# A two-block transformer kernel in three-product fp16: norm sums by token, one joint norm, pooling from the widest window down, and half of the gates' low part on ScalarE

## Chip, cores, metric

One core of one Trainium2 chip. The metric is device time in microseconds of one execution. The kernel is written at the level of engines: TensorE (PE), VectorE (DVE), ScalarE (ACT), GpSimd (POOL) and SyncE (SP), which starts most transfers. Each has its own program, and semaphores order them.

## What is computed

512 tokens of width 1024 go through two blocks, in fp32. Cut to what matters:

```python
# first block
h = concat(meta, x)                        # 16 + 512 tokens
proj = rmsnorm(h, ln1_w) @ w_in            # attention, gated linear attention
h = h + concat(attention, gla) @ w_out     # then the 512 tokens alone
hn = rmsnorm(h, ln2_w)
h = h + peer_ffn(hn)                       # top 16 of 128*128 experts, 8 heads, by token
x = rmsnorm(h, final_norm_w)               # "final1"
# second block
h = rmsnorm_2(x, mix_norm)                 # "mixn"
z = h @ w_in_2                             # pool, u, v and two gates, 1024 columns each
y_a = pool_mixer(z_pool) @ w_branch_a      # mean over the last 2, 4, 8, 16 tokens by channel group
y_b = (gelu(u) * (ws @ rmsnorm_2(gelu(v)) + b)) @ w_branch_b
x = x + (g_a * y_a + g_b * y_b) @ w_out
x = x + conv_ffn(rmsnorm_2(x, ffn_norm))   # "ffnn"
x = x + sigmoid(rmsnorm_2(x, ple_norm) @ w_gate) * (p @ w_ple)   # "plen"
return rmsnorm_2(x, final_norm)            # "final2"

rmsnorm(x, w) = x * rsqrt(mean(x*x, axis=-1) + 1e-6) * w
pool_mixer:  group g of 256 channels, w = (2, 4, 8, 16)[g]:
             (sum of the last w tokens) / min(t+1, w) - z, then @ w_pool[g], * pool_scale
```

## The kernel before

**Layout.** X holds the residual stream with channels on the 128 partitions: 8 chunks (c) of 128 channels, tokens along the free side (512, or 528 with the meta tokens). Weights come in slabs of 128x1024 fp32 through a ring of four (`wraw`): ScalarE cuts each to its fp16 high part (`cut_high`, L498), VectorE to the low part (`cut_low`, L511); in the expert part GpSimd takes the low cut for a while. Both ask for slab n+3 before they handle what slab n gave. A product of fp32 quality is three fp16 products, high by high, high by low, low by high (`parts`, L537 to L539). A chunk of a projection is 24 of them, 512 columns wide.

**Norms** (`class Norm`). ScalarE squares the chunks (L393) and loads the root's table ahead of the last one. TensorE sums over channels: with `ones` as weights and the squares moving (ln1, L421, L422), or for the others with `strip` as weights, which puts the sums of token tile t on rows 32t to 32t+31 (L426), four products of 128 columns a chunk. ScalarE takes the root (L400), on 128x128 or, for ln1, 128x528. VectorE takes the reciprocal (L452, L455), TensorE spreads it over all partitions (L445; not for ln1), and VectorE scales X (L461), from which ScalarE copies the high part (L406) and VectorE takes the low (L467). For ln2, ffnn and final2 GpSimd adds the squares of the first six chunks beforehand (L438). The final norm of block one writes X itself, and the first norm of block two starts from its squares.

**Experts.** All 128x128 experts are computed densely for 384 tokens, in 128 slabs; 128 tokens' picks are gathered instead. The matrix of gates is built in 48 octets of tokens, in six tile turns of eight octets and five slabs each: VectorE writes one-hot codes of column and row (`hot_slab`, `hot_row`, L2061, L2062) and the first times the gate's high and low half (L2064, L2065), in two buffers used in turn; TensorE multiplies them (`gate_octet`, L1119, L1120), ScalarE copies the result out (L1603), and at the end of a turn starts the store of 4096 KB to `gate_matrix`. Between octets TensorE takes half slabs (`spilled`), whose Gelu ScalarE writes (L1561). Then groups of four value slabs are accumulated in all eight banks of PSUM (`expert_output`); the last slab's products of chunk c are followed by a transpose of the gathered tokens' sum (L1148), and VectorE adds bank c to X (L2159).

**After it.** Norms final1 and mixn, then eight pool projections (`N_POOL`), four slabs of pool weights (`N_WP`), eight of gating values v in two halves (`N_SV`), eight of u (`N_SU`). A pool chunk c is evicted by ScalarE (L1672) into one of two buffers, GpSimd adds c//2+1 shifted copies (L2373), VectorE divides, subtracts and cuts (L2180 to L2184, L2170, L2171); ScalarE's next eviction but one waits for that. The pooled products' outputs are evicted and cut in the same way (L1679, L1682, L2191). SP's queue starts all slab transfers in order, with two small weights behind the end of final1.

What sets the order is the text of the five programs alone; nothing reorders them.

Of the kernel before, what the change touches and what calls it, by code (L numbers as in the profile page):

```python
# [49 lines left out]
N_WP = N_POOL + 8  # L50
N_SV = N_WP + 4
N_SU = N_SV + 8
# [69 lines left out]
def build(nc, io, out):  # L122
# [3 lines left out]
    with ctx:  # L126
# [32 lines left out]
        strip = base.take(P + 96)  # L159
# [164 lines left out]
        consts_in, vecs_in, ones_in, meta_in = sem("consts_in"), sem("vecs_in"), sem("ones_in"), sem("meta_in")  # L324
# [42 lines left out]
        POOLED, FIRST = ("ln2", "ffnn", "final2"), 6  # L367
        squares_added = sem("squares_added")
        NORMS = ("ln1", "ln2", "final1", "mixn", "ffnn", "plen", "final2")
# [5 lines left out]
        class Norm:  # L375


            def __init__(self, name, b):
                self.i = NORMS.index(name)
                self.b = b  # L380
                self.w, self.meta = VEC[name], name == "ln1"
                self.cut = name not in ("final1", "final2")
                self.nth = sum(n not in ("final1", "final2") for n in NORMS[:self.i])
                self.cols = TM if self.meta else T

                self.pooled = POOLED.index(name) if name in POOLED else None
                self.sq = nsq1 if self.meta else xsq if name == "final1" else nsq
                self.std = nstd1 if self.meta else nstd
                self.inv = ninv1 if self.meta else ninv

            def square(self, c):

                nc.scalar.activation(self.sq[:, c, 0:self.cols], X[:, c, 0:self.cols],  # L393
# [4 lines left out]
            def act(self, act, meanwhile=lambda: None):  # L398
                act.wait_ge(ss_done, self.i + 1)
                nc.scalar.activation(self.std, bank(self.b, TM if self.meta else P), ACT.Sqrt, bias=EPSC,  # L400
                                     scale=1.0 / D).then_inc(std_done, 1)
                meanwhile()
                if self.cut:
                    for c in range(KC):
                        act.wait_ge(xn_done, self.nth * KC + c + 1)
# [3 lines left out]
            def sum(self, pe, c):  # L409
# [3 lines left out]
                if self.pooled is not None and c < FIRST:  # L413
                    if c < FIRST - 1:
                        return
                    pe.wait_ge(squares_added, (self.pooled + 1) * (FIRST - 1))
                    c, first = 0, True
                else:
                    pe.wait_ge(sq_act, self.i * KC + c + 1)
                if self.meta:  # L420
                    nc.tensor.matmul(bank(self.b), ones, self.sq[:, c, 0:T], start=c == 0, stop=c == KC - 1)  # L421
# [347 lines left out]
        def _(pe):  # L769
# [394 lines left out]
            for c in range(KC):  # L1164
                n3.sum(pe, c)
# [1330 lines left out]
```

## Time and profile before

| | |
|---|---|
| median of 3 runs | 2467.96 us (2465.28 to 2469.02) |
| the profiled execution | 2466.73 us |
| its span | 2465.0 us |
| busy: PE, DVE, ACT, POOL | 95%, 69%, 43%, 25% of the span |
| HBM traffic | 190 GB/s over the span |

How to read the rows further down. In a timeline a row is: start and length in us, engine (PE is a product, SPq and ACTq a transfer's issue), line, operation, output<-input, shapes, xN for N in a row; in brackets the idle time before and who ended it. A list by line ends in the count, then busy us, mean ns | idle before, releaser. A row of one line's instructions gives ns min/median/max, then first and last start. A row of windows is the stretch, its length, then busy us (count) of PE, PE's weight loads, DVE, ACT, POOL, then the mean granted clock of TensorE (1.00 is 2.4 GHz), the DMA engines' share and GB/s. An fp32 product appears as two PE instructions.

### The profile page before, as it was taken

To read this page: it belongs to the slowest core of one execution; us is meant where nothing else is said; L and a number is where in the kernel's file an instruction comes from. 1 tells how busy PE (TensorE), PEld (TensorE's weight loads), DVE (VectorE), ACT (ScalarE), POOL (GpSimd) and SP (SyncE) were. 2 spreads that over 40 slices of the span, in tenths; PEclk is the share of its full clock that TensorE was granted. 3 is DMA by queue.
4 is the path that set the end of the run, shared out by engine and by line. 5 is a ranking of instruction groups with operands and counts; after the bars stand their busy time and mean duration, and the time that the engine had idled before them with its cause. 6 is when DMAs were issued, how large, how long until landed. Compare 5 with 4: busy or idle time off the path is not lost.

```text
span 2465.0 us, 38176 instructions
## 1 busy us (share of the span) xinstructions
PE 2336.5 (95%) x13568; PEld 1302.4 (53%) x13568; DVE 1707.9 (69%) x2979; ACT 1050.0 (43%) x1496; POOL 612.7 (25%) x494
## 2 busy tenths in 40 slices
PE   7998788999999998989999999988999999999998
PEld 3446664555555566655555555563454444443453
DVE  5326674568899989987888888878353438777235
ACT  4255333565666664543333333344422224333234
POOL 0003361277677651123322222204000010000001
PEclk9998999999999999999999999999999999999999
DMA  5200003378788778889999999923233323332321
GB/s 177 77 26 1 1 1 102 124 263 302 279 302 319 253 226 320 331 305 362 389 361 362 359 362 362 363 95 94 86 112 103 101 77 105 102 102 94 103 85 52
DMA packets 164871, 470.79 MB, mean 191 GB/s; under 512 B 17616, under 2 KB 70736, under 8 KB 163984
## 3 DMA queue, kind: packets, MB, share of 16 engines
q1 hardware_dynamic: 109312, 289.59, 34.3%
q0 software_dynamic: 36864, 134.23, 14.8%
q10 hardware_dynamic: 18576, 45.36, 4.9%
q8 instruction: 77, 1.26, 0.2%
q14 instruction: 42, 0.34, 0.0%
HBM read 421.67 MB, written 47.45 MB: 190 GB/s over the span
## 4 chain that ended last, share of the span: by engine, by line
PE 74%; DVE 14%; issue 4%; POOL 3%; ACT 2%; DMA 2%; DVEq 1%; SPq 0%; POOLq 0%; ACTq 0%
PE psum L537 23%; PE psum L538 23%; PE psum L539 23%; DVE arena L2026 3%; POOL arena L682 2%; PE psum L426 1%; DMA arena<-in_urows,arena 1%; DVE arena L2064 1%; DVE arena L511 1%; DVE arena L2061 1%; DVE arena L2065 1%; POOL arena L517 1%; DVEq L1951 1%; DVE arena L1868 0%; POOL arena L2335 0%
## 5 line engine op out<-in xcount | busy, mean ns | idle before, releaser
L537 PE MATMUL psum<-arena 128*128 128x384 f16 (+3 forms) x3648 | 1261.5, 347 | 34.2 <-DVE arena L467 13.2
L538 PE MATMUL psum<-arena 128*128 128x384 f16 (+3 forms) x3648 | 1264.6, 347 | 0.0
L539 PE MATMUL psum<-arena 128*128 128x384 f16 (+3 forms) x3648 | 1258.0, 346 | 0.0
L537 PEld LDWEIGHTS psum<-arena 128*128 128x128 f16 (+1 forms) x3648 | 354.1, 97 | 366.0 <-issue 50.5
L539 PEld LDWEIGHTS psum<-arena 128*128 128x128 f16 (+1 forms) x3648 | 353.9, 97 | 324.0 <-issue 8.1
L538 PEld LDWEIGHTS psum<-arena 128*128 128x128 f16 (+1 forms) x3648 | 353.6, 97 | 312.0 <-issue 8.4
L511 DVE SCALAR_TENSOR_TENSOR arena<-arena 128x1024 f16<-128x1024 f32 x216 | 267.4, 1240 | 307.9 <-ACT arena L498 307.4
L498 ACT ACTIVATE arena<-arena 128x1024 f16<-128x1024 f32 x216 | 226.4, 1050 | 259.5 <-PE psum L539 243.0
L1619 ACT ACTIVATE arena<-arena 128x1024 f16<-128x1024 f32 x128 | 135.3, 1057 | 298.9 <-PE psum L539 282.8
L517 POOL TENSOR_TENSOR arena<-arena 128x1024 f16<-128x1024 f32 x104 | 214.7, 2064 | 108.3 <-ACT arena L506 106.6
L2335 POOL DMA_INDIRECT arena<-in_v,arena x128 | 133.0, 1039 | 355.4 <-DVE arena L2037 323.6
L438 POOL TENSOR_TENSOR arena<-arena 128x512 f32<-128x512 f32 x15 | 19.8, 1320 | 760.3 <-ACT arena L393 760.3
L2335 POOL DMA_INDIRECT arena<-in_urows,arena x128 | 133.8, 1046 | 213.2 <-DVE arena L2026 156.3
L2026 DVE CUSTOM_DVE_ANT_0 arena<-arena,psum 128x1024 f32<-128x1024 f32 x128 | 151.3, 1216 | 26.4 <-DMA arena<-in_urows,arena 25.0
L2037 DVE SCALAR_TENSOR_TENSOR arena<-arena 128x1024 f32<-128x1024 f32 x126 | 161.0, 1280 | 0.0
L2111 DVE SCALAR_TENSOR_TENSOR arena<-arena 128x1024 f16<-128x1024 f32 x128 | 156.1, 1220 | 0.0
L1561 ACT ACTIVATE arena<-psum 128x384 f32<-128x384 f32 x128 | 62.8, 491 | 168.1 <-PE psum L539 160.4
L2105 DVE TENSOR_TENSOR arena<-arena 128x384 f16<-128x384 f32 x128 | 71.4, 558 | 63.0 <-ACT arena L1624 60.4
L504 ACT ACTIVATE arena<-arena 128x1024 f16<-128x1024 f32 x104 | 109.0, 1048 | 10.5 <-DMA arena<-in_w 9.9
L506 ACT ACTIVATE arena<-arena 128x1024 f32<-128x1024 f32 x104 | 110.0, 1058 | 3.3
L682 POOL TENSOR_TENSOR arena<-arena 64x256 f32<-64x256 f32 x72 | 63.3, 879 | 95.6 <-ACT arena L1456 92.2
L1727 ACT ACTIVATE arena<-psum 128x512 f32<-128x512 f32 x44 | 26.3, 598 | 142.5 <-PE psum L539 142.5
(254 smaller groups left out, 2236.9 us busy)
## 6 DMA issues: line engine op xcount, KB each, us to landing
arena<-in_w SPq DMA_DIRECT2D x320, 512.0 KB
arena<-in_v SPq DMA_DIRECT2D x128, 512.0 KB
early_activations<-arena ACTq DMA_DIRECT2D x124, 192.0 KB
arena<-early_activations SPq DMA_DIRECT2D x124, 192.0 KB
gate_matrix<-arena ACTq DMA_DIRECT2D x5, 4096.0 KB, 16.0
arena<-gate_matrix SPq DMA_DIRECT2D x32, 640.0 KB
arena<-in_xT SPq DMA_DIRECT2D x4, 512.0 KB, 5.5
arena<-in_urows,arena POOLq DMA_INDIRECT x128
```

The costliest lines, as they stand in the source:

```text
L498: nc.scalar.activation(wh[:, s, :], wraw[:, s, :], ACT.Copy, scale=WS).then_inc(high_cut, 1)
L511: nc.vector.scalar_tensor_tensor(out=wl[:, s, :], in0=wraw[:, s, :], scalar=WS, in1=wh[:, s, :], op0=ALU.mult, op1=ALU.subtract).then_inc( ...
L517: nc.gpsimd.tensor_tensor(wl[:, s, :], wraw[:, s, :], wh[:, s, :], ALU.subtract).then_inc(low_cut, 1)
L537: nc.tensor.matmul(ps, a_h, b_h, start=first, stop=False)
L538: nc.tensor.matmul(ps, a_h, b_l, start=False, stop=False)
L539: return nc.tensor.matmul(ps, a_l, b_h, start=False, stop=last)
L682: do.tensor_tensor(blocks(dst[li][rows, :], s, sd), blocks(src[rows, h, 0:T], s, sd), blocks(e[rows, :], s, sd), ALU.mult).then_inc(done, 1)
L1619: nc.scalar.activation(vh[:, s, :], vraw[:, s, :], ACT.Copy, scale=WS).then_inc(vhigh_cut, 1)
L2026: nc.vector.tensor_tensor_reduce(out=x, in0=x, in1=own_tok, scale=1.0, scalar=0.0, op0=ALU.mult, op1=ALU.add, accum_out=own_dot[:, k:k + 1 ...
L2037: ins = nc.vector.scalar_tensor_tensor(out=to, in0=x, scalar=by, in1=to, op0=ALU.mult, op1=ALU.add)
L2111: nc.vector.scalar_tensor_tensor(out=vl[:, s, :], in0=vraw[:, s, :], scalar=WS, in1=vh[:, s, :], op0=ALU.mult, op1=ALU.subtract).then_inc( ...
L2335: nc.gpsimd.indirect_dma_start(own_row(b, k >= PICKS), None, table, bass.IndirectOffsetOnAxis(own_at[:, k % PICKS:k % PICKS + 1], 0)).then ...
```

## The change

- **Sums by token.** The squares are now the weights and a table of a few columns (`pick`) moves: the sums of token tile t land with tokens on the partitions in column t. Roots and reciprocals are of 128x4 (128x5 for ln1, 128x8 joint), and the spread uses the reciprocal's column as broadcast weights with the identity moving. ln1, which had no spread, gets one; VectorE adds its squares 3 to 7. `pick` and the identity are loaded ahead of the other x, `ones` behind.
- **A joint norm.** From x = h*r1*w1 the second norm's moment is r1^2 * mean(h^2 w1^2): both means come from one pass over the squares of h, with two columns a tile (`wpick`). VectorE forms s1+eps and eps*(s1+eps)+s2 and their reciprocals, ScalarE one root of the eight. X is scaled with both at once for mixn; the scaling for the residual follows later, in the first step of the pooling loop.
- **Dealt sums.** The sums of chunk c-2 follow chunk c's products of the last value slab.
- **Pooling descending**: channel group 3 (window 16, four shifted sums) first; the first half of the gating values is placed between the pool projections and the pooled products, and the pooled products' outputs use another buffer (U2).
- **The gates' low part.** VectorE writes the first four tokens of an octet, ScalarE the other four with one scaled copy each (`low_half`), one octet ahead; TensorE waits for both.

```diff
@@ Norm @@
+        ADDED = {"ln1": (3, 7), "ln2": (0, 5), "ffnn": (0, 5), "final2": (0, 5)}
...
             def act(self, act, meanwhile=lambda: None):
-                act.wait_ge(ss_done, self.i + 1)
-                nc.scalar.activation(self.std, bank(self.b, TM if self.meta else P), ACT.Sqrt, bias=EPSC,
-                                     scale=1.0 / D).then_inc(std_done, 1)
+                if self.double:
+                    act.wait_ge(std_done, self.i + 1)
+                    nc.scalar.activation(self.inv, self.std, ACT.Sqrt).then_inc(inv_done, 1)
+                else:
+                    act.wait_ge(ss_done, self.i + 1)
+                    nc.scalar.activation(self.std, bank(self.sums, self.n), ACT.Sqrt, bias=EPSC,
+                                         scale=1.0 / D).then_inc(std_done, 1)
...
-                    for t in range(TT):
-                        last = nc.tensor.matmul(bank(self.b, P), strip[:, 96 - 32 * t:96 - 32 * t + P],
-                                                self.sq[:, c, t * P:(t + 1) * P], start=first and t == 0,
-                                                stop=c == KC - 1 and t == TT - 1)
...
+                for t in (0, *range(TT, self.tiles), *range(1, TT)):
+                    rows = P if t < TT else M
+                    w = wpick[:, c, 6 - 2 * t:14 - 2 * t] if self.double else pick[:, TT - t:TT - t + self.n]
+                    last = nc.tensor.matmul(bank(self.sums, self.n)[0:rows], self.squares[:, c, t * P:t * P + rows], w,
+                                            start=first and t == 0, stop=end and t == TT - 1)
...
+            def spread(self, pe):
+
+                pe.wait_ge(inv_done, self.i + 1)
+                for at, b in ((TT, self.b), (0, self.b - 1)) if self.double else ((0, self.b),):
+                    for t in range(self.tiles):
+                        rows = P if t < TT else M
+                        last = nc.tensor.matmul(psum[:, b * 512 + t * P:b * 512 + t * P + rows],
+                                                self.inv[0:rows, at + t:at + t + 1].to_broadcast([rows, P]),
+                                                ident[0:rows, 0:rows], start=True, stop=True)
+                    last.then_inc(spread_done, 1)
...
+                if self.double:
+                    dve.wait_ge(ss_done, self.i + 1)
+                    s1, s2 = (bank(self.sums, self.n)[:, j:self.n:2] for j in range(2))
+                    dchain.link(nc.vector.tensor_scalar(moments[:, 0:TT], s1, EPS, None, ALU.add))
+                    dchain.link(nc.vector.scalar_tensor_tensor(out=moments[:, TT:2 * TT], in0=moments[:, 0:TT], scalar=EPS,
+                                                               in1=s2, op0=ALU.mult, op1=ALU.add))
+                    nc.vector.reciprocal(self.std, moments).then_inc(std_done, 1)
@@ TensorE @@
...
                 pe.wait_ge(hot_out, e + 1)
+                pe.wait_ge(low_out, e + 1)
...
                         nc.tensor.transpose(bank(c, P, ND), own_sum[0][:, cols], ident).then_inc(own_turned, 1)
+                        if c >= 2:
+                            n4.sum(pe, c - 2)
...
-            n3 = Norm("final1", 0)
-            for c in range(KC):
-                n3.sum(pe, c)
-            n3.spread(pe)
-
-            n4 = Norm("mixn", 7)
-            for c in range(KC):
+            for c in (KC - 2, KC - 1):
                 n4.sum(pe, c)
             n4.spread(pe)
...
+            pe.wait_ge(final1_out, KC)
+            gating_values(N_SV)
+            pe.wait_ge(zpool_out, KC)
+            for n in range(N_WP, N_SV2):
...
+            pe.wait_ge(v_out, TT)
+            gating_values(N_SV2)
@@ ScalarE @@
+            def low_half(e):
+
+                b = e % 2
+                act.wait_ge(hot_slab_out, e + 1)
+                wait(act, g_done, e * 2 - 2)
+                for j in range(OCT // 2, OCT):
+                    tok = e * OCT + j
+                    last = nc.scalar.activation(hot_low[b][:, j // QUAD, :, j % QUAD],
+                                                hot_slab[b][:, j // QUAD, :, j % QUAD], ACT.Copy,
+                                                scale=idxT[:, 2, tok:tok + 1])
+                last.then_inc(low_out, 1)
+
+            low_half(0)
...
                     cuts.upto(N_U + e + (i + i // 4 + (i % 4 == 3)) // 2 + 3)
+                    if t * OCT + i + 1 < GT * OCT:
+                        low_half(t * OCT + i + 1)
@@ VectorE @@
+            n1.add_squares(dve, nc.vector)
...
-            cuts.upto(2)
-            n1 = Norm("ln1", 0)
-            n1.dve(dve)
+            cuts.upto(1)
+            n1.dve(dve, meanwhile=lambda: cuts.upto(2))
...
-                nc.vector.tensor_tensor(hot_low[b], hot_slab[b], col(gatel), ALU.mult).then_inc(hot_out, 1)
+                half = OCT // QUAD // 2
+                nc.vector.tensor_tensor(hot_low[b][:, 0:half], hot_slab[b][:, 0:half], col(gatel)[:, 0:half],
+                                        ALU.mult).then_inc(hot_out, 1)
...
+            for n in range(N_POOL, N_SV):
+                p, c = n - N_POOL, N_SV - 1 - n
                 cuts.upto(n + 3)
...
+                if n == N_POOL:
+                    dve.wait_ge(spread_done, n4.i + 2)
+                    for cc in range(KC):
+                        nc.vector.scalar_tensor_tensor(out=X[:, cc, 0:T], in0=X[:, cc, 0:T], scalar=f1[:, cc:cc + 1],
+                                                       in1=bank(n4.b - 1), op0=ALU.mult,
+                                                       op1=ALU.mult).then_inc(final1_out, 1)
```

The order of the instructions at two places, L numbers being those of each version's own lines. First TensorE at the end of the last value slab, before the change; L537 to L539 are products, L1148 the transpose, L426 sums, L445 spreads:

```order
L537 MATMUL psum<-arena 128x384
L538 MATMUL psum<-arena 128x384
L539 MATMUL psum<-arena 128x384
L1148 MATMUL psum<-arena 128x128
L426 MATMUL psum<-arena 128x128 x32
L445 MATMUL psum<-arena 128x128 x4
L426 MATMUL psum<-arena 128x128 x32
L445 MATMUL psum<-arena 128x128 x4
L537 MATMUL psum<-arena 128x512
```

And with the change, where L553 to L555 are the products, L1170 the transpose, L434 sums and L454 spreads:

```order
L434 MATMUL psum<-arena 128x8 x4
L553 MATMUL psum<-arena 128x384
L554 MATMUL psum<-arena 128x384
L555 MATMUL psum<-arena 128x384
L1170 MATMUL psum<-arena 128x128
L434 MATMUL psum<-arena 128x8 x12
L454 MATMUL psum<-arena 128x128 x8
L553 MATMUL psum<-arena 128x512
```

Four sums of each earlier chunk now stand before the next chunk's products, twelve behind the last transpose, and the second pass of 32 is gone.

Second ScalarE in the first tile turn, before: L1603 copies gates out, L1550 stores an activation, L1561 is the Gelu, L498 the high cut:

```order
L1603 ACTIVATE arena<-psum 128x128x4 x4
L1550 DMA early_activations<-arena 128x384
L1561 ACTIVATE arena<-psum 128x384
L498 ACTIVATE arena<-arena 128x1024
L1603 ACTIVATE arena<-psum 128x128x4 x2
```

And with the change, L1621 being the scaled copies, L1639 the gates out, L514 the cut:

```order
L1621 ACTIVATE arena<-arena 128x128 x4
L514 ACTIVATE arena<-arena 128x1024
L1621 ACTIVATE arena<-arena 128x128 x4
L1639 ACTIVATE arena<-psum 128x128x4 x2
L1621 ACTIVATE arena<-arena 128x128 x4
L1639 ACTIVATE arena<-psum 128x128x4 x2
```

Each octet's gates are copied out behind the scaled copies for the octet after it.

## Rows read from the trace of the kernel before

**Rows 1.** The page, part 4: the chain that ended last, its share by engine.

```profile
PE 74%; DVE 14%; issue 4%; POOL 3%; ACT 2%; DMA 2%; DVEq 1%; SPq 0%; POOLq 0%; ACTq 0%
```

**Rows 2.** TensorE's waits: who was waited for, us in total, times, longest.

```profile
PE psum L1119 <- DVE arena L2065: 19.9, 23, 1.6
PE psum L537 <- DVE arena L2191: 5.1, 1, 5.1
```

**Rows 3.** The timeline of the start: start us, length us, instruction, [idle before <-releaser].

```profile
10.83 0.15 DVE L1787 TENSOR_TENSOR arena<-arena 64x2 f32<-64x2 f32 x1 [10.83 <-DMA arena<-in_vec]
12.57 0.63 ACT L393 ACTIVATE arena<-arena 128x528 f32<-128x528 f32 x1
16.22 0.29 PE L422 MATMUL psum<-arena 128*128 128x16 f32 x2
17.30 0.29 PE L422 MATMUL psum<-arena 128*128 128x16 f32 x2
18.71 0.70 ACT L400 ACTIVATE arena<-psum,arena 128x528 f32<-128x528 f32 x1 [2.68 <-PE psum L422]
19.45 3.45 DVE L452 RECIPROCAL arena<-arena 128x528 f32<-128x528 f32 x1 [1.67 <-ACT arena L400]
22.94 1.45 DVE L461 SCALAR_TENSOR_TENSOR arena<-arena 128x528 f32<-128x528 f32 x2
25.27 0.58 PE L537 MATMUL psum<-arena 128*128 128x512 f16 x1 [6.29 <-DVE arena L467]
```

**Rows 4.** The tile stage: one turn's busy times, VectorE's L2065, ScalarE's copies by shape.

```profile
955.40:987.00 31.60, 28.25 (x252) 19.34 (x250) 30.77 (x48) 15.89 (x26) 5.72 (x5) 1.00 0.89 330
...
L2065 DVE TENSOR_TENSOR arena<-arena x48: 678/685/2481, 896.2 to 1088.7; 128x1024 f16<-128x1024 f16 x48
...
L1603 ACT ACTIVATE arena<-psum 128x512 f32<-128x512 f32 x80 | 44.8, 617 | 22.4 <-PE psum L1120 22.4
L1561 ACT ACTIVATE arena<-psum 128x384 f32<-128x384 f32 x25 | 12.3, 491 | 36.2 <-PE psum L539 34.9 <-issue 1.3
```

**Rows 5.** The lines L400, L455, L2194: duration ns min/median/max.

```profile
L400 ACT ACTIVATE arena<-psum,arena x7: 367/368/702, 18.7 to 2453.9; 128x128 f32<-128x128 f32 x6, 128x528 f32<-128x528 f32 x1
...
L455 DVE RECIPROCAL arena<-arena x6: 952/953/954, 446.1 to 2454.3; 128x128 f32<-128x128 f32 x6
...
L2194 DVE RECIPROCAL arena<-arena x1: 180/180/180, 1775.5 to 1775.5; 128x4 f32<-128x4 f32 x1
```

**Rows 6.** The timeline between the last expert slab and the pool projections.

```profile
1634.44 7.31 PE L426 MATMUL psum<-arena 128*128 128x128 f32 x64
1635.42 1.28 ACT L373 ACT_TABLE_LOAD   x1
1643.19 1.16 PE L445 MATMUL psum<-arena 128*128 128x128 f32 x8 [1.45 <-DVE arena L455]
1644.39 5.36 DVE L461 SCALAR_TENSOR_TENSOR arena<-arena,psum 128x512 f32<-128x512 f32 x8 [1.25 <-PE psum L445]
1655.91 1.41 DVE L461 SCALAR_TENSOR_TENSOR arena<-arena,psum 128x512 f32<-128x512 f32 x2 [1.25 <-PE psum L445]
```

**Rows 7.** The pooling part: windows, lines L2171 and L2373, and the timeline.

```profile
1670.90:1767.20 96.30, 89.24 (x393) 38.82 (x392) 59.62 (x67) 37.77 (x50) 26.59 (x21) 0.95 0.34 108
1716.70:1729.00 12.30, 12.30 (x46) 5.05 (x47) 7.93 (x10) 6.10 (x10) 0.00 (x0) 0.79 0.46 144
...
L2171 DVE TENSOR_TENSOR arena<-arena x46: 691/693/1644, 1675.0 to 2270.8; 128x512 f16<-128x512 f32 x26, 128x512 f32 x20
...
L2373 POOL TENSOR_TENSOR arena<-arena x20: 1062/1270/1916, 1671.6 to 1708.7; 128x527 f32<-128x527 f32 x8, 128x525 f32<-128x525 f32 x6, 128x521 f32<-128x521 f32 x4, 128x513 f32<-128x513 f32 x2
...
1697.13 1.23 DVE L511 SCALAR_TENSOR_TENSOR arena<-arena 128x1024 f16<-128x1024 f32 x1
1703.87 1.23 DVE L511 SCALAR_TENSOR_TENSOR arena<-arena 128x1024 f16<-128x1024 f32 x1
...
1704.59 0.39 PE L537 MATMUL psum<-arena 128*128 128x512 f16 x1 [2.00 <-ACT arena L1672]
```

More of the change, by code:

```diff
@@ L366, in build @@
         xn_done, xh_done, xl_done = sem("xn_done"), sem("xh_done"), sem("xl_done")
-        POOLED, FIRST = ("ln2", "ffnn", "final2"), 6
         squares_added = sem("squares_added")
-        NORMS = ("ln1", "ln2", "final1", "mixn", "ffnn", "plen", "final2")
+        NORMS = ("ln1", "ln2", "mixn", "ffnn", "plen", "final2")
+        ADDED = {"ln1": (3, 7), "ln2": (0, 5), "ffnn": (0, 5), "final2": (0, 5)}
         def roots_table(i):
@@ L441, in spread @@
-            def spread(self, pe):
-                pe.wait_ge(inv_done, self.i)
-                for t in range(TT):
-                    last = nc.tensor.matmul(bank(self.b, P, t * P), ident[:, 32 * t:32 * t + 1].to_broadcast([P, P]),
-                                            self.inv, start=True, stop=True)
-                last.then_inc(spread_done, 1)
-            def dve(self, dve, dst=None, done=None):
-                dve.wait_ge(std_done, self.i + 1)
-                if self.meta:
-                    dchain.link(nc.vector.reciprocal(self.inv, self.std))
-                    inv = self.inv
-                else:
+                end = c == KC - 1 or c == self.lo and self.hi == KC - 1
@@ L1136, in _ @@
                 spilled(e)
+            n4 = Norm("mixn", 7, sums=0)
             def expert_output(n, s, first=False, last=False):
@@ L1654, in _ @@
             cuts.upto(N_POOL + 2)
-            n3, n4 = Norm("final1", 0), Norm("mixn", 7)
+            n4 = Norm("mixn", 7, sums=0)
             for c in range(KC):
                 act.wait_ge(acc_out, c + 1)
-                n3.square(c)
-            n3.act(act)
-            for c in range(KC):
-                act.wait_ge(final1_out, c + 1)
                 n4.square(c)
@@ L1673, in _, with gating_values_out @@
                                      scale=ISW).then_inc(zpool_out, 1)
-            for n in range(N_WP, N_SV):
+            def gating_values_out(lo, half):
+                cuts.upto(lo + 7)
+                act.wait_ge(slab_done, lo + 4)
+                for t in range(TT):
+                    nc.scalar.activation(V2[:, 2 * t + half, :], bank(4 + t), ACT.Gelu,
+                                         scale=ISW).then_inc(v_out, 1)
+            gating_values_out(N_SV, 0)
+            for n in range(N_WP, N_SV2):
@@ L2160, in _ @@
                                                op0=ALU.mult, op1=ALU.add).then_inc(acc_out, 1)
-            Norm("final1", 0).dve(dve, dst=X, done=final1_out)
-            Norm("mixn", 7).dve(dve)
+            n4 = Norm("mixn", 7, sums=0)
+            n4.dve(dve)
             nc.vector.tensor_scalar(PSC, vec[:, VEC["pscale"]:VEC["pscale"] + KC], ISW, None,
```

250 lines of the change are left out of this document (129 added, 121 removed).

## The prediction

> **What bounds the kernel now.** I read the page first, then TensorE's waits, then the timeline of the four places that the change touches. The chain that ended last is 74% TensorE [rows 1], so a microsecond is worth something only where TensorE stands still, runs at half clock, or works for nothing. Its list of waits [rows 2] names two such places: 19.9 us in 23 waits before the gates' products (L1119, VectorE late), and one wait of 5.1 us in the pooling part. The other idle time is in the norms: at the start TensorE waits 6.29 us for the first operand [rows 3], and between the last expert slab and the pool projections the two norms take from 1634.44 until the second scaling starts at 1655.91 [rows 6], 21.5 us with no large product. In the tile stage [rows 4] VectorE is busy 30.77 of 31.6 us, ScalarE 15.89: VectorE sets that pace, ScalarE has half its time free.
>
> The sum is made against the profiled execution, 2466.73 us (span 2465.0 and 1.7 around it). The median of the runs, 2467.96, lies 1.2 higher; I add that at the end.
>
> **Part 1, the start: 4.2 us gained.** Before: last square done at 13.2, sums until 18.7, a square root over 528 columns (0.70), a reciprocal of 3.45 us, first scaling at 22.94 [rows 3]. A cycle there, 17.30-16.22 = 1.08 us, holds an fp32 product of 512 columns and one of 16, two instructions each. Of it 0.85 us is the 512 columns (2 instructions of 2 x 512 columns at 2.4 GHz); 0.23 is left for the two narrow ones, 0.117 each. I take 0.117 for every narrow fp32 instruction with new weights. After: VectorE gets its vectors at 10.8, does five tiny ones (0.8 us) and adds four squares (0.7 each), the last after the square at 13.2: 14.6. The sum product of 5 tiles is 10 instructions, 1.2 us: 15.8. Meanwhile VectorE does two slab cuts (2.3 us) until 17.0 and only then the reciprocal, 0.18 like the small one in [rows 5]. The spread is a step that was not there: 10 instructions of 1.16/8 = 0.145 [rows 6] and a start, 1.6 us, 18.7; the third cut (1.2 us) lies beside it. First scaling 18.75 instead of 22.94. The identity matrix is now asked for ahead of the remaining x (64 KB more in that queue, 0.2 us); the constants land long before the rotation that needs them. Bounds: 2.5 (cuts and adds late) and 6 (less half clock in the first products).
>
> **Part 2, the smaller norm operands: 3.6 us.** For ln2, ffnn, plen and final2 the reciprocal falls from 0.95 to 0.18 us on 128x4, the root from 0.37 to about 0.3 [rows 5]; 0.85-0.9 us each, times 4, all of it between the sums and the spread where TensorE stands. The sums themselves stay: 8 narrow instructions of 0.117 are 0.94 us, and 64 instructions took 7.31 us before, 0.914 per chunk [rows 6]. Bounds 2.5 and 4.5.
>
> The first rows show that what limits the new sums is the weight load, since the columns are gone. The Trainium skill, "TensorE: Matmul & The Clock Gate", section "Weight-path perf modes", says that fast weight load does not apply to fp32, and the section on LDWEIGHTS gives P/1.2 ns, 107 ns for 128 columns. By that rule a chunk's sums cost 0.86 us instead of 0.94, and turning the squares into weights buys nothing on TensorE.
>
> **Part 3, the joint norm: 11.1 us.** Now the eight chunks' sums start at 1634.44 and end at 1641.75, TensorE-bound; with them between the products the same work is there. Each chunk of the last slab takes 0.60 us (three products of 384 columns at 2.4 GHz, 0.48, and a transpose, 0.12) plus 0.94 of sums from the third on. Sum 0 waits for its square (0.4 us). Chunk 7's transpose then ends near 1639.5, sum 5 at 1640.5, accumulation and square of chunk 7 come behind the table load of 1.28 us [rows 6] at 1641.5, and the last sum ends at 1642.5. **Dealing the sums loses 0.8 us.** Three small VectorE operations (0.55), the root (0.3) and the first spread (1.2) follow: the scaling for mixn starts at 1644.8, where the one for final1 started at 1644.39. The second scaling started at 1655.91: 11.1 us less. What vanishes there is 5.36 us of scaling X, the second squares, 7.4 us of sums, root, reciprocal. The second spread (1.2 us) ends before the first low part of X is cut, and X's scaling (5.4 us) moves behind the cuts, into the time before the first window sum is out. Bounds 9.5 and 12.5.
>
> **Part 4, the gates' low part: 9.5 us.** VectorE's fourth operation takes 0.685 us for 1024 columns [rows 4]; less the overlap of neighbours (eight scalings of 0.74 in 5.36 us [rows 6], so 0.08) its pitch is 0.60, and 0.33 for 512, so 0.27 times 48 octets = 13 us less on VectorE. ScalarE gets four of 128 columns. Its price: 0.617 us for 512 and 0.491 for 384 columns [rows 4] give 0.24 for 128; the root with a pointer operand on 128x128 takes 0.37 [rows 5]; neighbours overlap by about 0.08 again. I take 0.30, 1.2 us a group, 9.6 a tile turn: 25.5 of about 29.8 us. At the first octet ScalarE reaches its group only after the preceding slab's Gelu: 1.2-1.9 us lost once. TensorE's own work bounds a turn: 31.6 less 19.9/6 = 3.3 of waits [rows 2, 4] is 28.3; VectorE's 30.77 less 2.16 is 28.6. With both that close they will wait for each other in turn, as VectorE's 0.83 us of idle time shows already, so I take 29.8 a turn; 1.8 times 6, less 1.3. Bounds 0 and 12. Two more things queue: behind ScalarE's new wait for the slab one-hots stand its gate copies and the Gelu, which have two octets of slack in banks; DMA at a share of 0.89 [rows 4] would be 0.95.
>
> By the Trainium skill, "ScalarE: Activation LUTs", section "Rules for kernel authors", multiplication belongs on VectorE. The rows bear it out, 1.2 us for what costs 0.27, and applied to a path through ScalarE it would cost 0.93 times 48 = 45 us. The trace's idle half of ScalarE is why I don't follow it.
>
> **Part 5, pooling in descending order: 4.2 us.** Before, TensorE lost 2.00 us [rows 7] and 5.1 [rows 2]; after each the granted clock fell to 1.2 GHz for a while (a mean of 0.79 over 1716.7 to 1729). In all the stage lasts 96.3 us from 1670.9, where the first pair is done, to the last values' eviction, for 6 projections of 5.2, 4 pooled slabs of 2.6 and 8 value slabs of 5.2, 82.8 us: 13.5 us too many, some 4 of them from the clock. The second wait goes: 20.7 us of gating products now cover the last chunks' pooling. But the chunks with three and four steps come first, when POOL and VectorE slow each other: a subtraction of 0.69 us takes 1.64, and VectorE's loop is 6.74 us long (1697.13 to 1703.87) against 5.2 of products (24 of 512 columns). That loop holds the low cuts of the slabs. With the pair done at T, an eviction (0.7) and four of POOL's steps of 1.27 are out at T+6, VectorE's first chunk at T+11.5, the cut of the fifth slab at T+12.7; TensorE wanted it at T+10.4. Walking on: waits of 2.4, 1.4, 1.0, 0.5 and 0.2, 5.5 us; 2.1 at the pooled products, where ScalarE's Gelu of the values stands before its evictions; 1.7 for one more spell at half clock. 9.3 against 13.5. Bounds -2 and 9.
>
> Measured, POOL's steps stretch from 1.06 to 1.9 us and VectorE's 0.69 to 1.64 [rows 7]. The Trainium skill, "SBUF — State Buffer", section "SBUF: two separate sides", calls the shared port pair an exclusive lock: the loser waits a whole instruction. By it each of VectorE's three long operations can wait up to 1.3 us, 6.1 us a chunk where I have 5.55 (6.74 less the cut's 1.2), and the sum of waits would be 7.7 us.
>
> **Sum.** 4.2+3.6+11.1+9.5+4.2 = 32.6; 2466.7-32.6 = 2434.1, plus 1.2: **2435.3**.
>
> **Rivals.**
> - *The tile stage gives nothing.* ScalarE is strictly in order; if the group for octet i+1 comes late, TensorE waits for it instead. For: five cuts, sixteen copies and five Gelus a turn share the queue. Against: VectorE's own hot_high is out no sooner. Time: 2435.3+9.5 = 2445. Chance 0.17.
> - *ScalarE becomes the bound: slower.* A turn is 15.9 us plus 32 operations. At 0.49 us each it equals today's 31.6; to eat the other 23.1 us a turn must grow by 3.9, which decides at (31.6+3.9-15.9)/32 = 0.61 us. At 0.75, twice the 128x128 row, a turn is 39.9: 8.3 times 6 less 23.1, 2495. Against: no row of 128 columns is above 0.37, and the strided copies (L1603, 0.617 for 512) stand in line with the plain ones (0.491 for 384) [rows 4]. Chance 0.04.
> - *Pooling keeps all its waits*, by the port lock of the skill's page or because the early stalls hold the clock at 1.2 GHz longer: 2435+4 to 6, 2440. Chance 0.14.
> - *The narrow sums are cheap*: if a narrow fp32 instruction costs half, 0.06, each dealt chunk saves 0.47, 3 us at the joint norm and 1.5 elsewhere: 2430. Chance 0.1.
> - *It doesn't do what it says*: the merged norm's chain waits elsewhere and gives 0. Against: two scalings in rows are one now. 2446. Chance 0.02.
>
> **Numbers.** My case has 0.53. The range reaches to 2422 (upper bounds of parts 4 and 5 together) and 2448 (both at their lower). A measurement of this kernel can tell about 0.2%, 5 us, from no change; only the ScalarE rival and several lower bounds at once lie there: faster 0.94, same 0.02, slower 0.04.
>
> **What would show it.** Right: first large product at 21, not 25.3; tile turns of 29.3 to 30 us; first product after the joint norm 11 us earlier relative to the last slab; X's scaling beside POOL; TensorE's waits in pooling for slab cuts, early. Wrong: the scaled copies above 0.4 us, TensorE waiting on ScalarE at the gates, a turn above 31, or a pooling stage no shorter.

## The result, and the profile after

The changed kernel takes 2454.11 us (median of 4 runs, 2450.03 to 2454.61) beside 2467.78 for the one before on the same chip: a ratio of 0.9942, 95% interval 0.9925 to 0.9959. It is faster, but by 14 us and not by 32; it lies above my range. The profiled execution has a span of 2452.7 us against 2465.0.

The page of the changed kernel, part 4, answers to [rows 1]: what left TensorE's share went to VectorE's.

```profile
PE 72%; DVE 16%; issue 4%; POOL 3%; ACT 2%; DMA 2%; DVEq 1%; SPq 0%; POOLq 0%; ACTq 0%
```

To see where the time went I lined up the third product of each triple (L539 before, L555 after, 3648 of each) and took the difference of their starts at the same count. "Lead" is how many us the changed kernel is ahead there.

| up to (time before) | lead, profiled | lead, its second profile | lead forecast |
|---|---|---|---|
| 39, first slab done | 1.4 | 2.9 | 4.2 |
| 581, ln2 done | 0.6 | 2.7 | 5.1 |
| 838, picks nearly done | -2.0 | -0.4 | 5.1 |
| 907, first octet | -4.1 | -2.5 | 3.8 |
| 1091, tile stage | 2.1 | 3.7 | 14.6 |
| 1630, last value slab | 1.1 | 2.7 | 14.6 |
| 1664, joint norm and half the first pair | 14.9 | 16.1 | 25.7 |
| 1743, pooling | 21.3 | 22.4 | 29.9 |
| 2276, ffnn | 18.6 | 23.6 | 30.8 |
| 2405, plen | 12.0 | 16.9 | 31.7 |
| 2465, the end | 12.3 | 16.8 | 32.6 |

The joint norm and pooling gave more than forecast; the start, the tile stage and the small norms gave less, plen lost 6.7, and a stretch that the change doesn't touch (581 to 838) lost 2.6 to 3.2. From 1743 to 2276 the two profiles of one kernel differ by 3.9 us (2.7 lost, 1.1 gained): a lead of a microsecond or two can be noise.

**Plen is the plainest.** Its timeline and then its windows, columns as in [rows 4]:

```profile
2370.33 11.39 PE L434 MATMUL psum<-arena 128*128 128x4 f32 x64 [1.45 <-ACT arena L399]
...
2381.58 0.59 PE L553 MATMUL psum<-arena 128*128 128x512 f16 x1
...
2386.66 1.07 PE L454 MATMUL psum<-arena 128*128 128x128 f32 x8
```

```profile
2370.00:2372.00 2.00, 1.67 (x15) 1.67 (x16) 2.00 (x5) 2.00 (x4) 0.00 (x0) 1.00 0.00 0
2372.00:2374.00 2.00, 2.00 (x16) 2.00 (x15) 1.79 (x4) 1.98 (x5) 0.00 (x0) 0.75 0.00 0
2374.00:2376.00 2.00, 2.00 (x11) 2.00 (x11) 0.00 (x0) 1.99 (x4) 0.00 (x0) 0.50 0.00 0
```

The same timeline before, not shown ahead:

```profile
2388.79 7.41 PE L426 MATMUL psum<-arena 128*128 128x128 f32 x64 [1.45 <-ACT arena L393]
...
2396.03 0.38 PE L537 MATMUL psum<-arena 128*128 128x512 f16 x1
```

TensorE is busy without a gap, yet while it runs through products with four moving columns the granted clock falls from 1.00 to 0.50 (1.2 GHz). At that clock a narrow instruction takes 0.18 us (11 in 2.00 us) instead of 0.117, and the 12 large products behind run at 0.63 instead of 0.38.

**The norm of ln2** answers to [rows 5]:

```profile
444.50 0.26 ACT L410 ACTIVATE arena<-psum,arena 128x4 f32<-128x4 f32 x1 [1.15 <-PE psum L434]
444.79 0.18 DVE L469 RECIPROCAL arena<-arena 128x4 f32<-128x4 f32 x1 [2.10 <-ACT arena L410]
445.03 2.08 PE L454 MATMUL psum<-arena 128*128 128x128 f32 x8 [0.57 <-DVE arena L469]
```

```profile
444.50:446.00 1.50, 0.97 (x4) 0.98 (x5) 0.18 (x1) 0.26 (x1) 0.00 (x0) 0.50 0.87 366
```

Root and reciprocal are as short as forecast, but the spread takes 2.08 us where it took 1.16: the clock is already at 0.50, where before it still stood at 1.00 during the spread.

**The start** answers to [rows 3], with slow sums and a slow spread again. The trace has no clock record before 28.1 us here, and the windows print 1.00 in its place; that the clock was low is read from the lengths, 0.58 to 0.63 us for a large product until 27.8:

```profile
8.10 5.97 PE L434 MATMUL psum<-arena 128*128 128x5 f32 x30 [8.10 <-ACT arena L399]
...
15.50 2.11 PE L434 MATMUL psum<-arena 128*128 128x5 f32 x10 [1.43 <-DVE arena L445]
...
18.19 2.61 PE L454 MATMUL psum<-arena 128*128 128x128 f32 x10
...
20.84 1.44 DVE L477 SCALAR_TENSOR_TENSOR arena<-arena,psum 128x528 f32<-128x528 f32 x2 [0.72 <-PE psum L454]
...
23.16 0.58 PE L553 MATMUL psum<-arena 128*128 128x512 f16 x1 [2.37 <-DVE arena L483]
```

**The tile stage** answers to [rows 4]: one turn, then VectorE's waits over 4.7 turns.

```profile
966.55:997.02 30.47, 28.28 (x250) 19.03 (x248) 28.71 (x48) 25.95 (x59) 5.72 (x5) 1.00 0.92 348
```

```profile
DVE arena L527 <- ACT arena L514: 9.1, 10, 1.9
```

VectorE fell to 28.71 and ScalarE rose to 25.95, as forecast (28.6, 25.5), but the turn is 30.47: VectorE stands 1.76 us, most of it once a turn in front of a slab's low cut.

**The joint norm** answers to [rows 6], **pooling** to [rows 7]:

```profile
1640.10 1.06 PE L434 MATMUL psum<-arena 128*128 128x8 f32 x8 [0.39 <-ACT arena L399]
...
1642.08 3.37 PE L454 MATMUL psum<-arena 128*128 128x128 f32 x16 [0.93 <-ACT arena L407]
1643.78 1.41 DVE L477 SCALAR_TENSOR_TENSOR arena<-arena,psum 128x512 f32<-128x512 f32 x2 [2.00 <-PE psum L454]
...
1646.07 0.38 PE L553 MATMUL psum<-arena 128*128 128x512 f16 x1 [0.62 <-DVE arena L483]
...
1668.36 0.38 PE L553 MATMUL psum<-arena 128*128 128x512 f16 x1 [1.39 <-DVE arena L527]
...
1674.16 0.38 PE L553 MATMUL psum<-arena 128*128 128x512 f16 x1 [0.46 <-DVE arena L527]
...
1679.96 0.38 PE L553 MATMUL psum<-arena 128*128 128x512 f16 x1 [0.45 <-DVE arena L527]
...
1717.87 0.38 PE L553 MATMUL psum<-arena 128*128 128x512 f16 x1 [1.44 <-DVE arena L2242]
...
1721.29 0.38 PE L553 MATMUL psum<-arena 128*128 128x512 f16 x1 [0.66 <-DVE arena L2242]
```

### The profile page after: what moved, and what is told of

Read it like the earlier page. It is cut to its first block, busy times and chain, and to the rows that moved or that the text cites. A ratio compares the mean times of both kernels' runs of the same rounds, so it can differ in the third digit from the quotient of the medians.

```text
span 2452.7 us, 38327 instructions
## 1 busy us (share of the span) xinstructions
PE 2341.5 (95%) x13522; PEld 1307.5 (53%) x13522; DVE 1696.3 (69%) x2989; ACT 1103.8 (45%) x1678; POOL 632.1 (26%) x494
## 4 chain that ended last, share of the span: by engine, by line
PE 72%; DVE 16%; issue 4%; POOL 3%; ACT 2%; DMA 2%; DVEq 1%; SPq 0%; POOLq 0%; ACTq 0%
PE psum L553 22%; PE psum L554 22%; PE psum L555 22%; DVE arena L2068 4%; POOL arena L699 2%; DVEq L1993 1%; DMA arena<-in_urows,arena 1%; PE psum L434 1%; PE psum L1139 1%; PE psum L1140 1%; DVE arena L527 1%; DVE arena L2004 1%; DVE arena L2006 1%; DVE arena L2007 1%; DVE arena L477 0%
## 5 line engine op out<-in xcount | busy, mean ns | idle before, releaser
L553 PE MATMUL psum<-arena 128*128 128x384 f16 (+3 forms) x3648 | 1263.3, 348 | 28.2 <-issue 8.9
L555 PE MATMUL psum<-arena 128*128 128x384 f16 (+3 forms) x3648 | 1259.0, 347 | 0.0
L553 PEld LDWEIGHTS psum<-arena 128*128 128x128 f16 (+1 forms) x3648 | 354.8, 97 | 362.6 <-issue 46.3
L555 PEld LDWEIGHTS psum<-arena 128*128 128x128 f16 (+1 forms) x3648 | 354.0, 97 | 324.7 <-issue 8.1
L514 ACT ACTIVATE arena<-arena 128x1024 f16<-128x1024 f32 x216 | 226.5, 1051 | 250.0 <-PE psum L555 234.6
L533 POOL TENSOR_TENSOR arena<-arena 128x1024 f16<-128x1024 f32 x104 | 228.2, 2195 | 97.6 <-ACT arena L522 96.5
L445 POOL TENSOR_TENSOR arena<-arena 128x512 f32<-128x512 f32 x15 | 19.8, 1319 | 763.0 <-ACT arena L399 763.0
```

Of the source, the lines that this page charges most:

```text
L514: nc.scalar.activation(wh[:, s, :], wraw[:, s, :], ACT.Copy, scale=WS).then_inc(high_cut, 1)
L533: nc.gpsimd.tensor_tensor(wl[:, s, :], wraw[:, s, :], wh[:, s, :], ALU.subtract).then_inc(low_cut, 1)
L553: nc.tensor.matmul(ps, a_h, b_h, start=first, stop=False)
L555: return nc.tensor.matmul(ps, a_l, b_h, start=False, stop=last)
```

## The experiments

### Is it the narrow sums that lose the clock?

Theory A: a run of products with four to eight moving columns does not hold TensorE's clock. Theory B: such a product is slow in itself. The table is repeated until 120 to 128 columns move; the squares stay the weights.

```diff
@@ Norm.sum @@
+                    wide = P // self.n
+                    w = w.unsqueeze(1).to_broadcast([P, wide, self.n])
-                    last = nc.tensor.matmul(bank(self.sums, self.n)[0:rows], ...
+                    last = nc.tensor.matmul(bank(self.sums, wide * self.n)[0:rows], ...
```

> Every sum product's moving table is repeated to 120 to 128 columns, so that as many columns move as before the change and the squares stay the weights. Theory A (a run of products with 4 to 8 moving columns does not hold TensorE's clock): plen's 64 take 7.4 us instead of 11.39 and the products behind them run at full clock, 8 to 9 us less together; ffnn 0.5 to 1; at the start the sums run at 0.117 us and the clock is up by the first large product, 2 to 4 us less. In all 11 to 13 us less than the changed kernel: 2442. Theory B (an fp32 product with the squares as weights is slow in itself, 0.178 us at any clock): nothing gained, 2454 or up to 3 more.

Measured: 2445.0 us (2439.78 to 2450.23), ratio to before 0.991, interval 0.9896 to 0.9925. Plen's timeline and windows:

```profile
2365.84 7.41 PE L437 MATMUL psum<-arena 128*128 128x128 f32 x64 [1.44 <-ACT arena L399]
...
2373.09 0.38 PE L557 MATMUL psum<-arena 128*128 128x512 f16 x1
```

```profile
2366.00:2370.00 4.00, 4.00 (x37) 4.00 (x38) 3.31 (x6) 3.98 (x7) 0.00 (x0) 1.00 0.00 0
2370.00:2374.00 4.00, 4.00 (x35) 3.51 (x34) 1.38 (x2) 2.61 (x5) 0.00 (x0) 1.00 0.00 0
```

Theory A holds: 7.41 us again, the clock at 1.00, and over plen 0.15 us lost instead of 6.7. The joint spread took 2.05 us instead of 3.37. One part missed: at the start the clock rose at 12.7 us but fell again at 16.1, and the last ten sums took 2.79 us; the time came out 3 us above the 2442 forecast.

Dealing taken away, first with narrow and then with wide tables:

```diff
@@ expert_output @@
-                        if c >= 2:
-                            n4.sum(pe, c - 2)
@@ behind it @@
-            for c in (KC - 2, KC - 1):
+            for c in range(KC):
                 n4.sum(pe, c)
```

> The joint norm's sums all stand behind the last value slab instead of between its chunks. By my prediction this costs nothing, even gains 0.8 us. Theory A: 64 products of 8 moving columns in a row are the case of plen again: about 2 us at full clock, the rest at half, 11.4 us in all from the last transpose instead of 5.5, then a spread at half clock and the first products too: the first pool product starts 5 to 7 us later relative to the first transpose than the 17.06 us of the changed kernel. Theory B (slow in itself at any clock) fell already by the dealt sums' 0.96 for 8, unless neighbours matter; it expects 7.4 us of sums.

> Both edits at once: every sum table 120 to 128 columns wide, and the joint norm's sums behind the last value slab. Undealt with narrow tables, the stretch from the first transpose of the last slab to the second chunk's product of the pool pair took 21.3 us against 17.6 dealt (narrow or wide). Theory A (the narrow sums lose the clock, dealing only hides that): with wide tables undealt sums run at 0.116 us each and the stretch is 16.5 to 17.8 us, as my prediction had it (dealing loses 0.8). Rival (the dealing itself gains, by filling TensorE's waits): 20 us or more.

Measured: 2460.92 us and 2439.8 us, one execution each. The joint sums of the two, narrow and then wide:

```profile
1637.98 10.99 PE L434 MATMUL psum<-arena 128*128 128x8 f32 x64
```

```profile
1629.40 7.31 PE L437 MATMUL psum<-arena 128*128 128x128 f32 x64
```

From the last slab's first transposed chunk to the third product of the pool pair, the stretch is 29.0 us before, 17.65 dealt and narrow, 17.6 dealt and wide, 21.3 undealt and narrow, 16.6 undealt and wide. The seven profiles with dealt narrow sums lie between 17.65 and 18.9, the three with dealt wide ones all at 17.6. The large products between the dealt sums hid most of the fault of the narrow tables, so that dealing gained 2.4 to 3.7 us there; without that fault dealing loses 1.0 us. (The narrow run's expectation of 5 to 7 us was too high; of its 2460.92, some 6 us are an unrelated stall between 840 and 907 us.) In the undealt wide one the start went as forecast: ten sums in 1.67 us, first large product at 21.80. The same 2 us of the start with wide tables, dealt and then undealt:

```profile
17.00:19.00 2.00, 2.00 (x9) 1.71 (x8) 1.15 (x2) 0.24 (x2) 0.00 (x0) 0.50 1.04 387
```

```profile
17.00:19.00 2.00, 1.61 (x13) 1.40 (x12) 1.37 (x3) 1.21 (x2) 0.00 (x0) 1.00 1.04 387
```

So at the start the wide tables let the clock rise in both, at 12.7 and 13.6 us. In the first TensorE then stood 1.49 us before its last ten sums, and the clock fell at 16.1; in the second it stood 0.48 and the clock held until 20.4. The rise has a price: the first thirty sums took 6.59 and 6.99 us with 125 moving columns and 5.97 with 5.

### What untouched stretch loses 3 us?

> The changed kernel unaltered, a second profile. Against the kernel before, its first profile lost 4.7 us of lead between 581 and 907 us, a stretch the change does not touch, 1.7 of it in a spell at half clock at 833.5 to 836.6. Theory (chance): the second profile has no such spell and the first gates' product starts 3 to 5 us earlier than the 909.4 of the first. Rival (the change shifts when transfers fall due): it starts within 1 us of 909.4 again and the spell is there. Both expect the sums of plen at 11.4 us for 64 instructions again, and half clock until 27.8 at the start.

> The kernel before unaltered, a second profile, as a yardstick for stretches the change does not touch. Of the changed kernel's profiles so far each loses 1.8 to 4.2 us against the first profile of before between 581 and 840 us. Theory (chance of that one profile): the second profile of before comes to the same place 2 to 4 us later than the first did, with a spell at half clock near 833. Rival (the change brings it about): within 0.5 us of the first profile.

Measured: 2450.0 and 2465.97 us. The first gates' product of the changed kernel started at 907.84, the spell was there again (831.9 to 834.5), plen's sums took 12.1 us, and half clock ended at 25.5, not at 27.8. The kernel before came to its place near 838 at 836.94, with no spell. That points to the change, though two profiles of each kernel are few. The one difference that I found on an engine was in an instruction that the change leaves alone, GpSimd's low cut of a slab, before and after:

```profile
L517 POOL TENSOR_TENSOR arena<-arena x104: 1993/2004/3014, 460.3 to 904.2; 128x1024 f16<-128x1024 f32 x104
```

```profile
L533 POOL TENSOR_TENSOR arena<-arena x104: 2138/2151/2868, 459.1 to 906.3; 128x1024 f16<-128x1024 f32 x104
```

The new small tables take 137 words where `strip` took 224, so every later tile moved by 348 bytes.

```diff
         moments = base.take(2 * TT)
+        base.take(87)
```

(7 in the second run.)

> The changed kernel with 87 words left free behind its new small tables, so that all later tiles lie at the addresses of the kernel before (the new tables take 137 words where the old one took 224). In the changed kernel GpSimd's 104 low cuts take 2.151 us (median) where they took 2.004, though neither the instruction nor its place was changed, and VectorE's last head turn takes 53.5 us instead of 51.75. Theory (the shift of the addresses by 348 bytes makes them slower): the cuts take 2.00 again, the turn 51.8, the product behind the pick stage (840 us in the changed kernel) comes 2 to 4 us sooner and ScalarE's copies of gates take 0.62 instead of 0.72: 2448 to 2451. Rival (another phase between GpSimd and VectorE is the cause): 2.15 and 53.5 stay, 2454.

> 7 words left free instead of 87: every later tile starts at a multiple of 32 bytes as before the change, but not at the old addresses. If it is alignment that counts, the cuts take 2.00 us and the last head turn 51.8 us as in the run with the old addresses; if it is which tiles lie where, they stay at 2.15 and 53.5.

Measured: 2448.63 us, ratio 0.9917 (0.9902 to 0.9931), and 2448.51 in one execution. With 7 words:

```profile
L534 POOL TENSOR_TENSOR arena<-arena x104: 1993/2005/2576, 459.2 to 903.0; 128x1024 f16<-128x1024 f32 x104
```

With 87 the median is 2003 ns. VectorE's last full head turn takes 51.7 us with 87 words and 51.8 with 7 instead of 53.5, the turn before it 51.1 and 51.0 instead of 52.6, and the copies of gates take 0.60 instead of 0.72. So it is alignment, not the place: tiles shifted by 348 bytes are slow, tiles shifted by 320 are not. As 320 is a multiple of 64 and 348 only of 4, the runs do not tell 8, 16, 32 and 64 bytes apart. With 7 words the product near 838 came at 836.8 and no lead was lost between 581 and there; with 87 it came at 840.8, after a spell at half clock at 678 of its own, so that part of the expectation failed there. How much of the loss up to 838 is the addresses' stays open: without padding it was 1.8 to 4.2 us in eight profiles and 9.2 in one, with padding 2.5, 2.9 and none. The intervals of the changed kernel and of this one just overlap (0.9925 and 0.9931): that the whole gains 5 us is likely, that the instructions are faster is shown.

### What holds the tile turn at 30.5 us?

> The gates' low part is all on VectorE again, the rest as changed. If the tile stage's gain is the low part's alone, a turn goes back from 30.46 to 31.57 us, and the stage from the first gates' product to the last is 6.2 to 6.7 us longer, 2460.5. If anything else had shortened the turn (the clock, transfers), it stays under 31.2. The first gates' product should also come 1.9 us sooner, since TensorE waits there for the scaled copies.

The edit puts VectorE's multiplication back on all eight tokens and takes `low_half` and TensorE's wait for it away. Measured: 2455.42 us; a turn is 31.54, and the stage has 0.06 us of gain left against before:

```profile
964.14:995.68 31.54, 28.11 (x249) 19.16 (x248) 30.73 (x48) 17.40 (x28) 5.74 (x5) 1.00 0.89 327
```

The first gates' product started without a wait, where the changed kernel waited 1.87 us. The whole came out 5 us under the 2460.5 forecast, with a lead of 5.4 us by 397 us that has nothing to do with the edit; a single execution's whole time is worth that little, the stage is worth its row.

```diff
@@ VectorE, tile_turn @@
+                    if i and i in TILE_DOTS:
+                        own_dots(picks + TILE_DOTS.index(i), 1)
                     if i:
                         cuts.upto(...)
...
-                    if i in TILE_DOTS:
+                    if i in TILE_DOTS and not i:
                         own_dots(picks + TILE_DOTS.index(i), 1)
```

> The changed kernel with one thing moved in the tile turns: VectorE takes the gathered tokens' dot product before the slab's low cut instead of behind it. Theory: the 1.76 us a turn that VectorE still stands idle (once a turn, 1.61 us before L527) is the wait for ScalarE's high cut, which waits for TensorE to leave the slab's slot; a dot product (1.2 us) fits into it, a turn falls from 30.46 to about 29.3 us, 6 turns 5 to 7 us: 2447. Rival (TensorE's own 28.3 and the scaled copies hold the turn together with VectorE): 30.2 or more, under 2 us in all.

Measured: 2443.96 us, a turn, then VectorE's waits in the same stretch as above:

```profile
963.42:992.75 29.33, 28.07 (x249) 19.10 (x248) 28.70 (x48) 25.82 (x59) 6.06 (x5) 1.00 0.95 359
```

```profile
DVE arena L527 <- ACT arena L514: 2.9, 7, 0.7
```

The wait was the ring of slabs: ScalarE's high cut waits for TensorE to leave the slot (at 982.34 in the changed kernel, after 2.11 us idle), VectorE's low cut for ScalarE. While VectorE was the slower this was hidden. The stage now gains 13.1 us against before instead of 6.2.

### Is it the order of the groups, or the cover?

The edit turns the eight pool slabs, the four of pool weights and four programs' loops round (`c = p`); the gating values stay where the change put them.

> Pooling from the narrowest window up again, all else as changed: the gating values still stand between the pool projections and the pooled products. From the first pair's last chunk to the last pooled product the changed kernel gained 6.4 us over the one before, with waits of 1.39, 0.46, 0.45 us for slab cuts and no half clock. Theory: the gain is the gating products' cover alone, the order of the groups is worth under 1.5 us. Rival (my prediction's account, in which the order moves the stalls): ascending, the last chunks' four steps delay TensorE's later slab cuts and a wait of 2 us (as in the rows 7) returns, with half clock behind it: 3 to 5 us.

Measured: 2453.81 us. TensorE's waits from the first pair to the gating values:

```profile
1693.72 0.39 PE L553 MATMUL psum<-arena 128*128 128x512 f16 x1 [0.95 <-DVE arena L527]
...
1701.24 0.39 PE L553 MATMUL psum<-arena 128*128 128x512 f16 x1 [2.16 <-DVE arena L527]
```

These are 3.1 us of waits late in the loop instead of 2.3 us early in it. The wait of 2 us that the rival foresaw came back, but no half clock behind it: the stage gains 5.7 instead of 6.4. So nearly all of the gain is there without the new order, which is worth 0.7. That the rest is the cover by the gating products is the likely reading; no run took the cover away, nor the second buffer (U2).

### A version that beats both

```diff
@@ TensorE @@
+            def warm(b, n):
+                half = ident.bitcast(f16)
+                for _ in range(n):
+                    nc.tensor.matmul(bank(b, 2 * P), half[:, 0:P], half[:, 0:2 * P], start=True, stop=True)
...
             n2.spread(pe)
+            warm(4, 26)
```

> A version that is meant to beat both: sum tables of 128 columns but for ln1, the dot product ahead of the cut as in dots_first, and junk fp16 products of 256 columns into a free bank while TensorE waits (12 before ln1's last sums, 18 behind its spread, 26 behind the spreads of ln2 and ffnn). Theory A on the clock: no spell at half clock behind ln2 and ffnn, 2 to 2.5 us each, 1 to 3 at the start; with the wide tables' 10 and the dots' 6 some 20 us less than the changed kernel: 2434. Rival (the clock falls at a norm whatever TensorE does): 2440.

> All that helped together: sum tables of 128 columns but for ln1, junk products while TensorE waits behind three norms, the dot product ahead of the slab cut, and the old addresses. The kernel without the last of them gave 2437.9. Theory: 2 to 5 us less, 2434. Rival (addresses don't matter): 2438.

Measured: 2437.93 us (ratio 0.9884, 0.9862 to 0.9905) and, with the old addresses, **2432.18** (0.9842, 0.9819 to 0.9865). The first forecast was 4 us too low, the second 2 too high. The two intervals overlap, so what the old addresses add here is not settled. The norm of ln2 in the last:

```profile
446.00:448.00 2.00, 2.00 (x21) 1.80 (x20) 1.64 (x3) 0.87 (x2) 0.00 (x0) 1.00 0.97 403
448.00:450.00 2.00, 2.00 (x16) 1.34 (x14) 2.00 (x4) 1.02 (x2) 0.00 (x0) 1.00 1.02 418
450.00:452.00 2.00, 2.00 (x11) 0.89 (x10) 2.00 (x4) 0.96 (x2) 0.00 (x0) 1.00 0.35 141
```

The clock stays at 1.00 where every kernel here without the junk products ran at 0.50 behind this norm; between 397 and 581 us the first of the two gained 2.5 us of lead. The junk isn't free: in both the first product came 0.50 us behind its operand instead of 0.15. At the start the clock rose at 16.6 us in the first of the two, but at 24.4 in the second, where the first large product came 1 us late behind the junk. And the lead did not last: in the first it fell from 8.1 us at 581 to 1.6 at 697, with two head turns of VectorE at 61.4 and 58.1 us instead of 58.2 and 54.9; what lengthened them stays open.

## Why the prediction was wrong, step by step

- **Part 1, start: 4.2 forecast, 2.1 at the first large product, 1.4 to 2.9 a slab later.** The step that failed: "I take 0.117 for every narrow fp32 instruction". That price came from a stretch in which 512-column products stood between. Alone they ran at 0.199 (30 in 5.97 us) and 0.21, and the spread of ten at 0.26: 0.9 us and 1.0 us more. VectorE's vectors came 1.0 later (11.82). Some 0.8 of these 2.9 us cost nothing, as VectorE's cuts were to hold the reciprocal until 17.0 anyway.
- **Part 2, small operands: 3.6 forecast, 0.1 at ln2 and a loss of 6.7 at plen.** Root and reciprocal went as priced. The term left out was the clock: 2.08 for 1.16 at the spread, and in plen 4 us of sums and 2.7 of large products at 1.2 GHz. I had counted the sums as "stay". The rule that I set beside it, P/1.2 ns for a weight load ("TensorE: Matmul & The Clock Gate", the Trainium skill, section on LDWEIGHTS), would have 0.107 for an instruction; the rows show 0.116 at the higher clock (64 in 7.41 us, with wide tables) and 0.18 at the lower.
- **Part 3, joint norm: 11.1 forecast, 11.4 to the first product and 13.8 with the pair behind it.** The mechanism was right. The 2.4 on top is the pair at full clock, where it was at half before. TensorE had stood 0.62 us before it instead of 2.32; that this is why is likely, not shown. "Dealing the sums loses 0.8" was right only for tables that hold the clock (1.0); with the change's own tables dealing gains 2.4 to 3.7.
- **Part 4, low part: 9.5 forecast, 6.2 less 2.1 at the first octet.** The copies cost 0.33 each (4 in 1.31) against my 0.30, VectorE came to 28.7 against 28.6, TensorE to 28.3. The term that failed is "29.8 a turn": 1.76 us of VectorE's waiting where I allowed 1.2, all of it the slot of the slab. I had named ScalarE's order as the danger; it was the ring. The loss at the first octet was 1.87 where I took 1.3. The rival in which ScalarE is the bound is out: 0.33 against the 0.61 from which it decides.
- **Part 5, pooling: 4.2 forecast, 6.4.** The second wait went, the pooled products' 2.1 came as written. The slab cuts cost 2.3 instead of 5.5 and there was no spell at half clock (1.7 forecast). Before, waits (7.1) and clock (4) in this stretch were some 11 us, not 13.5. By my estimate from the exclusive lock of "SBUF — State Buffer" (the Trainium skill, section "SBUF: two separate sides") it would have been 7.7 of waits; the rows show slabs 5.80 us apart for two chunks, between my 5.55 and its 6.1, and then no more waits.
- **Not in the prediction at all:** the addresses. Shown are 3.4 us on VectorE's last two full head turns and 1.0 to 1.2 us of lead between 1091 and 1630, lost in all nine profiles without padding and in none of the three with it; what of the 2.6 to 3.2 between 581 and 838 is theirs is open. A lead from before 581 mostly lasted: with undealt wide tables it was 4.7 us above the changed kernel's at 581 and 4.2 above it at 838. Only the lead of 8.1 us made with junk products went altogether, to -1.1.
- **The range** does not follow from its own bounds. The upper bounds of parts 4 and 5 together give 2428, not 2422, and both lower ones 2451, not 2448; the measured 2454.11 lies above either.
- The chances: "the narrow sums are cheap" was the wrong way round, and no rival had them dearer; 0.94 for faster was right. Parts 3 and 5 came out above their forecasts and made up for some of what the others lacked.

## What to carry to other kernels

A product that is bound by its weight load looks free to narrow; look at the granted clock of the stretch before believing it, and keep the table wide where it costs nothing (from a cold clock, at the start, it did cost). Price an instruction from a row in which its neighbours are those that it will have. When a bottleneck engine gets relief, ask what stood behind it unseen (here a slot of the slab ring), and after any change of a memory plan compare the duration of instructions that were not touched.

## What the runs showed that I had not expected

- TensorE without a gap at half clock: 64 fp32 products of four moving columns in 11.39 us (12.10 in the second profile) with the granted clock down to 0.50, the same 64 with 128 moving columns in 7.41 us at 1.00.
- 26 junk products of 256 columns in 3.00 us kept the clock at 1.00 over a norm and delayed the first product behind it by 0.35 us.
- GpSimd's 128x1024 low cut takes 2.151 us with its tiles shifted by 348 bytes and 2.003 to 2.005 at the old addresses or 320 bytes off them; ScalarE's 128x512 copy into a strided tile 0.717 and 0.602. ScalarE's plain 128x1024 cut stayed at 1.05 us.
- Tiny VectorE operations can take long beside GpSimd: the eight 128x128 conversions, one a head, took anything from 0.23 to 2.13 us in the changed kernel and from 0.23 to 2.75 before. That they wait for GpSimd's cut is argued from their overlap, not shown by a run.
